# Experts, spilled blocks, last norm, embedding gate and final norm as one program

## The chip, the cores and the metric

The kernel runs on one core of a Trainium2 chip. The core has TensorE (PE) for matmuls, VectorE (DVE) and ScalarE (ACT) for elementwise work, GpSimd (POOL), and SyncE (SP), which issues DMAs. Each engine follows its own queue of instructions; they meet at semaphores. Matmul results go to PSUM, eight banks of 128 x 512 f32. All other tiles are in SBUF, 128 partitions wide. The metric is the device time of one execution in microseconds; the verdict compares medians of runs.

## What is computed

The reference is a model of two blocks over 512 tokens of 1024 features. The first is a hybrid attention mixer and a SwiGLU; the second a gated mixer, a mixture of experts and an embedding gate. Only the end of the second matters here:

```
x = x + hier_moe(rmsnorm_2(x, g_ffn), w_grp, w_exp, w1, w3, w2)
h = rmsnorm_2(x, g_ple)
x = x + sigmoid(h @ w_pg) * (p @ w_ple)
return rmsnorm_2(x, g_final)
# rmsnorm_2(x, g) = x * rsqrt(mean(x * x) + 1e-6) * g
```

`hier_moe` sends each token to 2 of 32 experts; an expert is (silu(x w1) * (x w3)) w2, with 1024 x 512, 1024 x 512 and 512 x 1024 weights.

## The kernel before, in words

The kernel is a list of stages (`build`). A stage opens a `Block`, in which each engine has its own list of instructions, and ends with a barrier of all engines. P is 128, NT 4 tiles of 128 tokens, KD 8 tiles of 128 features, CH and U 512 columns, PAIRS 16. The residual x is in `reg_b` as four tiles of 128 tokens x 1024 features.

`stage_experts` goes through 16 pairs of experts, 64 tokens each. SP loads the six weight matrices of a pair (2 MB each) into eight buffers (`b.wbuf`); a buffer is loaded again when PE is through with it. For a pair PE computes h1 and h3, DVE and ACT the gated product, PE the second product (`ex_y`), ACT (`weigh_high`, L2639) and DVE (`weigh_low`, L2647) split its weighted value in two parts, PE sends them home to their tokens with a selection matrix (`send_home`, L2656 and L2657), and DVE adds the eight results to x (`add_home`, L2663). The stages are staggered: in turn s of the loop the first products of pair s and the second of pair s - 1 are made. Behind its last weights SP loads the gate's weights `w_pg` (two halves of 2 MB), the final norm's gain row, broadcast to all partitions, and copies the products p @ w_ple (`b.pw`, 2 MB, already in SBUF) to a buffer of the ring.

`stage_spill` serves experts with more than 64 tokens. How many blocks there are is data (`b.spill`). Each engine loads the count to a register and has the code for one block in a loop inside an `If`. With these inputs the trace shows no instruction of such a block.

`stage_norm` for "n5" squares x, takes root and reciprocal, scales the rows, turns them with 32 PE transposes (L515), and ACT and DVE take the eight turned tiles out of PSUM, scaled by the gain `g_ple` per feature (L473, L507).

`stage_embedding` computes h @ w_pg in two halves of 512 output columns. A product of f32 is made of three fp32r matmuls (`product_parts`, L546 to L548): high x high, high x low, low x high. ACT makes the high part by a cast (L590 for weights, L576 for rows), DVE the low part by a subtraction (`lower`, L541). The weights come in eight units of 256 features x 512 columns, in two buffers; a unit has 24 matmuls, six for each tile of tokens, 192 in all. After the fourth and the eighth unit ACT takes the sigmoid of four banks (L2976), and DVE multiplies by `pw` (L2987) and adds to x (L2989). In its list DVE does the four gated tiles of the first half ahead of the low part of the sixth unit.

`stage_final` squares the four tiles (L3002), takes one root and one reciprocal (L3005, L3012), scales each by its factor and by the gain row on DVE (L3015), and SP stores the four tiles (L3022).

An ACT_TABLE_LOAD comes ahead of a function that is not in the loaded set; here Sqrt needs one after the others, and Sigmoid one after Sqrt.

## Time and profile before

| | us |
|---|---|
| median of 3 runs | 1934.57 |
| lowest, highest | 1934.0, 1939.59 |
| the profiled execution, its own time | 1938.65 |
| its span, first to last instruction | 1936.9 |
| PE busy in it | 1740.1 (90%) |
| DVE, ACT busy | 807.0 (42%), 516.2 (27%) |
| moved by DMA | 353.69 MB, mean 183 GB/s |

The trace names each instruction by engine, line, and the tiles it writes and reads. PE and PEld are matmuls and weight loads; a matmul's end is modelled and overlaps the next one's start, so one should count starts. A "q" behind an engine's name is its instruction queue, where barriers stand: a DRAIN is the engine's arrival at a barrier, an EVENT_SEMAPHORE the release. Times run from the span's start. The span is 1.75 us shorter than the execution's own time.

### The profile page before, as it was taken

What the parts mean: (1) busy time and instruction counts of PE and PEld (TensorE: products, weight loads), DVE (VectorE), ACT (ScalarE), POOL (GpSimd) and SP (SyncE); (2) the same over time, 40 slices, a digit from 0 to 9 for tenths busy, and PEclk for the clock granted to TensorE, in tenths of its full rate; (3) what the DMA queues carried; (4) which work ended last, traced back from release to release, by engine and by line L of the source; (5) the groups of instructions that cost most, each with busy time, mean ns of one, the idle gap of its engine ahead of it and who ended that gap; (6) DMA issues with size and microseconds to landing.
All of it is one profiled execution on the core that took longest, in us unless ns stands there. A gap on an engine that the chain in (4) does not pass through costs nothing. (4 is left out here: it accounts for less than half of the span.)

```text
span 1936.9 us, 20199 instructions
## 1 busy us (share of the span) xinstructions
PE 1740.1 (90%) x8167; PEld 1189.8 (61%) x8167; DVE 807.0 (42%) x1266; ACT 516.2 (27%) x858; POOL 46.5 (2%) x86
## 2 busy tenths in 40 slices
PE   2999989899979999999799989998998888888865
PEld 2887856546768888788688776665333434333354
DVE  4663457632652222365622553345223323232343
ACT  4212257622242222222532340423100000000032
POOL 0000000100000000000000000000200000000000
PEclk8999999989989999999899999999999999999987
DMA  9664030022512332220431111255899999999901
GB/s 356 216 264 149 1 131 1 2 96 78 174 44 91 116 98 87 98 77 32 152 110 65 37 51 44 87 236 202 359 425 426 427 428 426 426 429 427 393 1 43
DMA packets 86216, 353.69 MB, mean 183 GB/s; under 512 B 8765, under 2 KB 38121, under 8 KB 70377
## 3 DMA queue, kind: packets, MB, share of 16 engines
q1 hardware_dynamic: 83562, 343.98, 45.2%
q0 software_dynamic: 2560, 8.40, 1.1%
q8 instruction: 66, 1.08, 0.2%
q14 instruction: 28, 0.23, 0.0%
HBM read 343.93 MB, written 6.33 MB: 181 GB/s over the span
## 5 line engine op out<-in xcount | busy, mean ns | idle before, releaser
L541 DVE TENSOR_TENSOR arena<-ring,arena 128x1024 fp32r<-128x1024 f32 x120 | 146.9, 1225 | 242.3 <-ACT arena L590 223.2
L546 PE MATMUL up_ps<-h_high,arena 128*128 128x512 f32 x352 | 139.1, 395 | 6.7 <-PEq L172 6.2
L547 PE MATMUL up_ps<-arena 128*128 128x512 f32 x352 | 139.7, 397 | 0.0
L548 PE MATMUL up_ps<-h_high,arena 128*128 128x512 f32 x352 | 139.6, 397 | 0.0
L590 ACT CAST arena<-ring 128x1024 fp32r<-128x1024 f32 x82 | 85.7, 1045 | 170.2 <-PE up_ps L548 88.5
L2632 PE MATMUL ex_h<-ring,u_big_tail 128*64 128x512 f32 x512 | 116.5, 603 | 13.1 <-DMA ring<-in_w 12.8
L2632 PE MATMUL ex_h<-s_ab,u_big_tail 128*64 128x512 f32 x400 | 114.7, 596 | 11.8 <-DMA reg_a<-in_w 4.9
L2603 DVE TENSOR_TENSOR u_big_tail<-ex_x,vcol 128x512 f32<-128x512 f32 x32 | 20.6, 686 | 185.8 <-PE ex_x L2596 185.8
L2837 ACT ACTIVATE u_big_tail<-ex_h 128x512 f32<-128x512 f32 x16 | 9.6, 597 | 305.6 <-PE ex_h L2632 305.6
L2632 PEld LDWEIGHTS ex_h<-ring,u_big_tail 128*64 128x64 f32 x512 | 38.8, 138 | 76.5 <-issue 75.3
L546 PEld LDWEIGHTS up_ps<-h_high,arena 128*128 128x128 f32 x352 | 66.5, 189 | 23.4 <-issue 6.6
L2632 PEld LDWEIGHTS ex_h<-s_ab,u_big_tail 128*64 128x64 f32 x400 | 35.8, 137 | 73.3 <-issue 70.6
L547 PEld LDWEIGHTS up_ps<-arena 128*128 128x128 f32 x352 | 66.4, 189 | 16.3
L548 PEld LDWEIGHTS up_ps<-h_high,arena 128*128 128x128 f32 x352 | 66.5, 189 | 15.3
L546 PE MATMUL down_ps<-arena 128*128 128x512 f32 x176 | 68.6, 389 | 1.7 <-PEq L1767 1.7
L547 PE MATMUL down_ps<-arena 128*128 128x512 f32 x176 | 68.5, 389 | 0.0
L548 PE MATMUL down_ps<-arena 128*128 128x512 f32 x176 | 68.5, 389 | 0.0
L2632 PE MATMUL ex_y<-s_ab,u_big_tail 128*64 128x512 f32 x176 | 56.5, 594 | 13.3 <-DMA s_ab<-in_w 5.7
L2632 PE MATMUL ex_y<-ring,u_big_tail 128*64 128x512 f32 x256 | 56.6, 594 | 10.1 <-DMA ring<-in_w 10.1
L523 PE MATMUL merge_p<-s_ab,ring 128*128 128x512 f32 x128 | 59.5, 618 | 4.1 <-PEq L1162 3.1
L546 PE MATMUL p_ps<-p_h,p_w 128*128 128x512 f32 x128 | 51.8, 405 | 7.4 <-DVE p_h L541 6.8
L546 PE MATMUL p_ps<-arena,h_high 128*128 128x512 f32 x128 | 51.5, 402 | 7.6 <-PEq L172 7.6
(531 smaller groups left out, 3532.2 us busy)
## 6 DMA issues: line engine op xcount, KB each, us to landing
ring<-in_w SPq DMA_DIRECT2D x48, 2048.0 KB, 28.8
s_ab<-in_w SPq DMA_DIRECT2D x36, 2048.0 KB, 28.3
ring<-in_w_in SPq DMA_DIRECT2D x19, 2048.0 KB, 7.8
ring<-in_w_ada SPq DMA_DIRECT2D x24, 1024.0 KB, 6.7
reg_a<-in_w SPq DMA_DIRECT2D x12, 2048.0 KB, 32.1
ring<-in_w_ffn_gate SPq DMA_DIRECT2D x11, 1024.0 KB, 5.2
ring<-in_w_ffn_up SPq DMA_DIRECT2D x11, 1024.0 KB, 7.7
ring<-in_w_ffn_down SPq DMA_DIRECT2D x5, 2048.0 KB, 7.9
```

The costliest lines, as they stand in the source:

```text
L523: mm = nc.tensor.matmul(ps, w[:, k, n0:n0 + P], hT[:, k, :], start=(k == 0), stop=(k == kt - 1))
L541: return engine.tensor_tensor(lo, v, hi.bitcast(F32), ALU.subtract)
L546: nc.tensor.matmul(ps, x[0], y[0], start=start, stop=False)
L547: nc.tensor.matmul(ps, x[0], y[1], start=False, stop=False)
L548: return nc.tensor.matmul(ps, x[1], y[0], start=False, stop=stop)
L590: self.nc.scalar.copy(self.unit(u, 0), v).then_inc(self.hi, 1)
L2603: last = nc.vector.tensor_tensor(xT[:, 4 * i:4 * i + 4, :], ps[i][:].rearrange("p (k s) -> p k s", k=4), b.gcol[:, 4 * i:4 * i + 4, :], AL ...
L2632: mm = nc.tensor.matmul(ps[half, :], xT[:, k, half], ws[j][:, k, cols], start=(k == 0), stop=(k == k_end - 1))
L2837: nc.scalar.activation(b.hs, ps_h1[:], ACT.Silu).then_inc(silu, 1)
```

## The change

The stages for spilled blocks, the norm "n5", the embedding gate and the final norm become empty. Their work moves behind the pairs in the block of the experts, as the classes `Spill` and `Finish`. In short:

- Each engine loads the count of spilled blocks at the start of the loop's last turn. Behind its part of the pairs stands the same `If` over the same code as before. Where there are spilled blocks, ACT squares x again.
- SP loads the final gain row first, ahead of the experts' weights, into `scr`. The copy of `pw` goes. The two halves of `w_pg` have a semaphore each.
- The norm's gain `g_ple` goes into the weights: ACT's high part is a copy with a scale per partition, DVE's low part multiplies by it as well. The rows carry only the token's factor. ACT makes the high parts of the first two units and loads the table for Sqrt ahead of the squares.
- The squares are taken tile by tile as the experts' adds arrive. The scaled rows are turned and split tile by tile, out of PSUM: ACT the high part, DVE the low part. PE's first unit is mixed with the transposes.
- The low part of the sixth unit now stands ahead of the gated tiles of the first half. The last two units are done in the order (6,0) (6,1) (7,0) (6,2) (7,1) (6,3) (7,2) (7,3), unit and tile.
- For the final norm the squares of the first half are summed while the second half's products run, and there is a root for each tile. DVE multiplies by the gain row before the factor is known; the factor is then applied by DVE for tiles 2 and 3 and by ACT for tiles 0 and 1. They are stored in the order 2, 0, 3, 1.

```diff
 def stage_experts(b):
...
-    b.frow = b.wbuf[2][:, 0:D]
-    pw_home = b.wbuf[3].rearrange("p (t n) -> p t n", t=NT)
+    b.frow = b.scr[:, U:3 * U]
+    fin = Finish(b, pg)
...
+        spill = Spill(b, ps_x, [ps_h1, ps_h3], ps_y, [ps_t, ps_c])
+        fin.banks = [ps_h1, ps_h3, ps_t, ps_c] + ps_x + ps_y
         @block.sync
         def _(sp):
+            sp.dma_start(b.frow, a["g_final_2"].partition_broadcast(P)).then_inc(fin.row_in, 16)
             sp.wait_ge(b.ple_done, 2 * NT)
...
             sp.wait_ge(h1, PAIRS)
             for i in range(2):
-                sp.dma_start(pg[i], feature_tiles(...)[...]).then_inc(b.last_in, 16)
-            sp.wait_ge(y_done, PAIRS - 1)
-            sp.dma_start(b.frow, a["g_final_2"].partition_broadcast(P)).then_inc(b.last_in, 16)
-            sp.dma_start(pw_home, b.pw).then_inc(b.last_in, 16)
+                sp.dma_start(pg[i], feature_tiles(...)[...]).then_inc(fin.pg_in[i], 16)
+            spill.sync(sp, spill.count(sp))
+            fin.sync(sp)
         @block.gpsimd
         def _(pool):
+            nc.gpsimd.memset(fin.eps, EPS).then_inc(fin.eps_in, 1)
...
+            spill.pool(pool, spill.count(pool))
         @block.tensor
...
             for s in range(PAIRS + 1):
+                if s == PAIRS:
+                    n_spill = spill.count(pe)
...
+            spill.tensor(pe, n_spill)
+            fin.tensor(pe)
         @block.vector
...
             for s in range(PAIRS + 1):
+                if s == PAIRS:
+                    n_spill = spill.count(dve)
...
             add_all(PAIRS - 1)
+            spill.vector(dve, n_spill)
+            fin.vector(dve)
         @block.scalar
...
             for s in range(PAIRS + 1):
+                if s == PAIRS:
+                    n_spill = spill.count(act)
...
+            fin.first_weights(act)
+            for t in range(NT):
+                act.wait_ge(added, HOME * (PAIRS - 1) + 2 * t + 2)
+                last = fin.square(t)
+            last.then_inc(fin.squared, 1)
+            act.wait_ge(fin.squared, 1)
+            spill.scalar(act, n_spill, fin)
+            fin.scalar(act)
+class Spill:
...
+    def count(self, eng):
+        eng.wait_ge(self.b.spilled, 1)
+        return eng.value_load(self.b.spill[0:1, SPILL:SPILL + 1], min_val=0, max_val=SPILL)
+    def each(self, eng, n, body, after=None):
+        with eng.If(n > 0):
+            with eng.Fori(0, n) as j:
+                body(j)
+            if after is not None:
+                after()
...
+class Finish:
...
+    def act_w(self, act, u):
+        act.wait_ge(self.pg_in[u % 4 // 2], 16)
+        if u == 5:
+            act.wait_ge(self.ready, NT)
+        elif u >= 2:
+            act.wait_ge(self.used, u - 1 if u < 5 else u - 2)
+        for k in range(2):
+            v, g = self.weight(u, k)
+            last = self.nc.scalar.activation(self.w[u % 2][0][:, k, :], v, ACT.Copy, scale=g)
+        last.then_inc(self.w_hi, 1)
+    def dve_w(self, dve, u):
+        dve.wait_ge(self.w_hi, u + 1)
+        for k in range(2):
+            v, g = self.weight(u, k)
+            last = self.nc.vector.scalar_tensor_tensor(out=self.w[u % 2][1][:, k, :], in0=v, scalar=g,
+                                                       in1=self.w[u % 2][0][:, k, :].bitcast(F32), op0=ALU.mult, op1=ALU.subtract)
+        last.then_inc(self.w_lo, 1)
...
+    def first_weights(self, act):
+        self.act_w(act, 0)
+        self.act_w(act, 1)
+        act.wait_ge(self.eps_in, 1)
+        self.nc.scalar.activation(self.spare, self.eps, ACT.Sqrt)
+    def tensor(self, pe):
+        nc, b = self.nc, self.b
+        def turn(t):
+            pe.wait_ge((self.y_d, self.y_a)[t % 2], t // 2 + 1)
+            if t >= 2:
+                pe.wait_ge(self.lo, 2 * (t - 1))
+            for k in range(KD):
+                mm = nc.tensor.transpose(self.turn_bank(t, k // 4)[:, k % 4 * P:k % 4 * P + P], self.y[t][:, k * P:k * P + P], b.ident[:])
+                if k % 4 == 3:
+                    mm.then_inc(self.turned, 1)
+        def product(u, t):
+            pe.wait_ge(self.w_lo, u + 1)
+            i = u % 4
+            if u == 0:
+                pe.wait_ge(self.lo, 2 * t + 2)
+            for k in range(2):
+                mm = product_parts(nc, self.banks[u // 4 * NT + t][:], [self.h[j][:, 2 * i + k, t * P:t * P + P] for j in range(2)],
+                                   [self.w[u % 2][j][:, k, :] for j in range(2)], i == 0 and k == 0, i == 3 and k == 1)
+            if i == 3:
+                mm.then_inc(self.ready, 1)
+            return mm
+        turn(0)
+        turn(1)
+        product(0, 0)
+        turn(2)
+        product(0, 1)
+        turn(3)
+        product(0, 2)
+        product(0, 3).then_inc(self.used, 1)
+        for u in range(1, 6):
+            for t in range(NT):
+                mm = product(u, t)
+            if u != 3:
+                mm.then_inc(self.used, 1)
+        for u, t in ((6, 0), (6, 1), (7, 0), (6, 2), (7, 1), (6, 3), (7, 2), (7, 3)):
+            product(u, t)
+    def vector(self, dve):
+        nc, b = self.nc, self.b
+        def split(t):
+            for half in range(2):
+                dve.wait_ge(self.hi, 2 * t + half + 1)
+                ks = slice(4 * half, 4 * half + 4)
+                lower(nc.vector, self.h[1][:, ks, t * P:t * P + P], self.turn_bank(t, half)[:].rearrange("p (k s) -> p k s", k=4),
+                      self.h[0][:, ks, t * P:t * P + P]).then_inc(self.lo, 1)
+        def normed(t):
+            nc.vector.tensor_scalar(self.y[t], b.x[:, t, :], self.inv[:, t:t + 1], None, ALU.mult).then_inc(self.y_d, 1)
+        def gated(h, t):
+            i, cols = h * NT + t, slice(h * CH, h * CH + CH)
+            dve.wait_ge(self.gate, i + 1)
+            nc.vector.tensor_tensor(self.sg[:, i], self.sg[:, i], b.pw[:, t, cols], ALU.mult).then_inc(self.prod, 1)
+            dve.wait_ge(self.prod, i + 1)
+            nc.vector.tensor_tensor(b.x[:, t, cols], b.x[:, t, cols], self.sg[:, i], ALU.add).then_inc(self.added, 1)
+        self.dve_w(dve, 0)
+        dve.wait_ge(self.rooted, 1)
+        nc.vector.reciprocal(self.inv, self.root).then_inc(self.inverted, 1)
+        dve.wait_ge(self.inverted, 1)
+        normed(0)
+        normed(2)
+        self.dve_w(dve, 1)
+        for t in range(NT):
+            split(t)
+        for u in range(2, 6):
+            self.dve_w(dve, u)
+        for t in range(NT):
+            gated(0, t)
+        self.dve_w(dve, 6)
+        self.dve_w(dve, 7)
+        dve.wait_ge(self.sq0, NT)
+        nc.vector.tensor_scalar(self.low, self.ss0, 1.0 / D, EPS, ALU.mult, ALU.add).then_inc(self.gained, 1)
+        dve.wait_ge(self.row_in, 16)
+        for t in range(NT):
+            gated(1, t)
+            dve.wait_ge(self.added, NT + t + 1)
+            nc.vector.tensor_tensor(self.y[t], b.x[:, t, :], b.frow, ALU.mult).then_inc(self.gained, 1)
+        dve.wait_ge(self.rooted2, NT)
+        nc.vector.reciprocal(self.inv, self.root).then_inc(self.inverted2, 1)
+        dve.wait_ge(self.inverted2, 1)
+        dve.wait_ge(self.gained, NT + 1)
+        for t in (2, 3):
+            nc.vector.tensor_scalar(self.y[t], self.y[t], self.inv[:, t:t + 1], None, ALU.mult).then_inc(self.out_d, 1)
+    def scalar(self, act):
+        nc, b = self.nc, self.b
+        def normed(t):
+            nc.scalar.activation(self.y[t], b.x[:, t, :], ACT.Copy, scale=self.inv[:, t:t + 1]).then_inc(self.y_a, 1)
+        def split(t):
+            for half in range(2):
+                act.wait_ge(self.turned, 2 * t + half + 1)
+                nc.scalar.copy(self.h[0][:, 4 * half:4 * half + 4, t * P:t * P + P],
+                               self.turn_bank(t, half)[:].rearrange("p (k s) -> p k s", k=4)).then_inc(self.hi, 1)
+        def sigmoid(h, t):
+            i = h * NT + t
+            act.wait_ge(self.ready, i + 1)
+            nc.scalar.activation(self.sg[:, i], self.banks[i][:], ACT.Sigmoid).then_inc(self.gate, 1)
+        def half_square(h, t):
+            act.wait_ge(self.added, h * NT + t + 1)
+            nc.scalar.activation(self.sg[:, h * NT + t], b.x[:, t, h * CH:h * CH + CH], ACT.Square,
+                                 accum_out=(self.ss0, self.ss1)[h][:, t:t + 1]).then_inc((self.sq0, self.sq1)[h], 1)
+        nc.scalar.activation(self.root, self.ss, ACT.Sqrt, scale=1.0 / D, bias=self.eps).then_inc(self.rooted, 1)
+        act.wait_ge(self.inverted, 1)
+        normed(1)
+        split(0)
+        normed(3)
+        for t in range(1, NT):
+            split(t)
+        for u in range(2, 6):
+            self.act_w(act, u)
+        for t in range(NT):
+            sigmoid(0, t)
+        self.act_w(act, 6)
+        for t in range(NT):
+            half_square(0, t)
+        self.act_w(act, 7)
+        for t in range(NT):
+            sigmoid(1, t)
+        nc.scalar.activation(self.spare, self.eps, ACT.Sqrt)
+        act.wait_ge(self.gained, 1)
+        for t in range(NT):
+            half_square(1, t)
+            act.wait_ge(self.sq1, t + 1)
+            nc.scalar.activation(self.root[:, t:t + 1], self.ss1[:, t:t + 1], ACT.Sqrt, scale=1.0 / D,
+                                 bias=self.low[:, t:t + 1]).then_inc(self.rooted2, 1)
+        act.wait_ge(self.inverted2, 1)
+        act.wait_ge(self.gained, NT + 1)
+        for t in (0, 1):
+            nc.scalar.activation(self.y[t], self.y[t], ACT.Copy, scale=self.inv[:, t:t + 1]).then_inc(self.out_a, 1)
+    def sync(self, sp):
+        b, nc = self.b, self.nc
+        for t in (2, 0, 3, 1):
+            sp.wait_ge((self.out_a, self.out_d)[t // 2], t % 2 + 1)
+            sp.dma_start(b.out[0, t * P:(t + 1) * P, :], self.y[t]).then_inc(self.stored, 16)
+        sp.wait_ge(self.stored, 16 * NT)
 def stage_spill(b):
-    ...
+    return
 def stage_combine(b):
-    ...
+    return
 def stage_embedding(b):
-    ...
+    return
 def stage_final(b):
-    ...
+    return
```

## Rows read from the trace of the kernel before

**Rows 1.** The page's 40 slices of the span: DMA busy tenths, and GB/s:

```profile
DMA  9664030022512332220431111255899999999901
GB/s 356 216 264 149 1 131 1 2 96 78 174 44 91 116 98 87 98 77 32 152 110 65 37 51 44 87 236 202 359 425 426 427 428 426 426 429 427 393 1 43
```

**Rows 2.** Chain of waits: shares by line, then start us, us:

```profile
by line: ACT u_big L3002 0.2%; DVE u_big L3015 0.2%; ACT L3005 0.1%; DVEq L2998 0.1%; ACTq L2998 0.0%; DVE small L3012 0.0%; issue 0.0%
...
1921.69 4.27 ACT u_big L3002 x8
```

**Rows 3.** Instructions of L2684, the experts' barrier: duration ns, first and last start us:

```profile
L2684 ACTq EVENT_SEMAPHORE  x1: 17/17/17, 1844.0 to 1844.0; - x1
```

**Rows 4.** Instructions of L2855, the spilled blocks' barrier:

```profile
L2855 ACTq DRAIN  x1: 14/14/14, 1844.9 to 1844.9; - x1
...
L2855 DVEq DRAIN  x1: 19/19/19, 1845.3 to 1845.3; - x1
L2855 PEldq DRAIN  x1: 13/13/13, 1848.8 to 1848.8; - x1
```

**Rows 5.** Timeline of ACT from 1800: start us, us, instruction [idle before]:

```profile
1835.33 1.27 ACT L2639 ACTIVATE y_hi_tail<-ex_y,share 128x512 fp32r<-128x512 f32 x2 [23.42 <-PE ex_y L2632]
...
1851.30 1.28 ACT L467 ACT_TABLE_LOAD   x1
1852.59 0.21 ACT L467 ACTIVATE small<-small 128x4 f32<-128x4 f32 x1
...
1915.36 2.06 ACT L2976 ACTIVATE s_ab<-em_g 128x512 f32<-128x512 f32 x4 [9.78 <-PE em_g L548]
```

**Rows 6.** Timeline of DVE from 1800:

```profile
1827.42 0.68 DVE L2818 COPY u_big_tail<-ex_t 128x512 f32<-128x512 f32 x1
...
1843.06 0.68 DVE L2663 TENSOR_TENSOR reg_b<-reg_b,ex_x 128x512 f32<-128x512 f32 x1
```

**Rows 7.** Timeline of PE from 1818:

```profile
1825.63 0.63 PE L2760 MATMUL ex_t<-ident,u_big_tail 128*128 128x128 f32 x4
...
1841.66 0.39 PE L2657 MATMUL ex_x<-y_lo_tail,pick_tail 128*128 128x512 f32 x1
...
1864.90 0.77 PE L546 MATMUL em_g<-em_w,em_h 128*128 128x512 f32 x1 [5.42 <-DVE em_h L541]
...
1894.85 0.39 PE L548 MATMUL em_g<-em_w,em_h 128*128 128x512 f32 x1
1897.07 0.50 PE L546 MATMUL em_g<-em_w,em_h 128*128 128x512 f32 x1 [1.83 <-DVE em_w L541]
...
1914.93 0.39 PE L548 MATMUL em_g<-em_w,em_h 128*128 128x512 f32 x1
```

**Rows 8.** Windows: busy us of each engine, PEclk the granted clock:

```profile
1847.00:1848.00 1.00, 0.00 (x0) 0.00 (x0) 0.00 (x0) 0.00 (x0) 0.00 (x0) 0.58 0.00 0
1858.00:1859.00 1.00, 1.00 (x12) 1.00 (x11) 0.25 (x1) 0.14 (x1) 0.00 (x0) 1.00 0.00 0
1865.00:1871.00 6.00, 6.00 (x14) 4.66 (x15) 5.10 (x8) 2.92 (x5) 0.00 (x0) 0.50 0.00 0
1872.00:1894.00 22.00, 22.00 (x99) 18.22 (x98) 7.11 (x9) 7.43 (x9) 0.00 (x0) 1.00 0.00 1
1898.00:1902.00 4.00, 4.00 (x13) 3.10 (x12) 0.15 (x1) 0.00 (x0) 0.00 (x0) 0.57 0.00 0
```

**Rows 9.** Groups by line and form, 1835 to 1937: busy us, mean ns:

```profile
L497 DVE TENSOR_SCALAR u_big_tail<-reg_b,small 128x1024 f32<-128x1024 f32 x2 | 1.4, 751 | 0.0
L2647 DVE SCALAR_TENSOR_TENSOR y_lo_tail<-ex_y,share,y_hi_tail 128x512 fp32r<-128x512 f32 x2 | 1.4, 746 | 8.1 <-ACT y_hi_tail L2639 8.1
```

**Rows 10.** Timeline of SP from 1150:

```profile
1333.51 0.35 SPq L2573 DMA_DIRECT2D reg_a<-in_w  x1
1357.79 10.24 SPq L2573 DMA_DIRECT2D s_ab<-in_w  x3
...
1929.03 3.92 SPq L3022 DMA_DIRECT2D out<-u_big  x4
```

More of the change, by code:

```diff
@@ L415, in stage_norm @@
                residual_row=None, save=None):
-    if made is not None or name in ("n2", "n3", "n4"):
+    if made is not None or name in ("n2", "n3", "n4", "n5"):
         return
@@ L2992, in stage_final @@
-def stage_final(b):
-    nc = b.nc
-    y = b.u_big[:, 0:NT * D].rearrange("p (t d) -> p t d", t=NT)
-    ss = b.small[:, 0:4]
-    sq, var, root, inv, done, stored = (b.sem(f"fi_{n}") for n in ("sq", "var", "root", "inv", "done", "stored"))
-    with nc.Block() as block:
-        @block.scalar
-        def _(act):
-            for t in range(NT):
-                last = nc.scalar.activation(y[:, t, :], b.x[:, t, :], ACT.Square, accum_out=ss[:, t:t + 1])
-            last.then_inc(sq, 1)
-            act.wait_ge(var, 1)
-            nc.scalar.activation(ss, ss, ACT.Sqrt).then_inc(root, 1)
-        @block.vector
-        def _(dve):
-            dve.wait_ge(sq, 1)
-            nc.vector.tensor_scalar(ss, ss, 1.0 / D, EPS, ALU.mult, ALU.add).then_inc(var, 1)
-            dve.wait_ge(root, 1)
-            nc.vector.reciprocal(ss, ss).then_inc(inv, 1)
-            dve.wait_ge(inv, 1)
-            for t in range(NT):
-                nc.vector.scalar_tensor_tensor(out=y[:, t, :], in0=b.x[:, t, :], scalar=ss[:, t:t + 1], in1=b.frow,
-                                               op0=ALU.mult, op1=ALU.mult).then_inc(done, 1)
-        @block.sync
-        def _(sp):
-            for t in range(NT):
-                sp.wait_ge(done, t + 1)
-                sp.dma_start(b.out[0, t * P:(t + 1) * P, :], y[:, t, :]).then_inc(stored, 16)
-            sp.wait_ge(stored, 16 * NT)
```

247 lines of the change are left out of this document (120 added, 127 removed).

## The prediction

> **What bounds the kernel now.** I read the page's slices first: from slice 29 to 37 the DMA engines are busy 9 tenths and more [rows 1]. That is the experts' weights coming in. There the kernel is bound by DMA, at some 426 GB/s in the second row; but in slice 38 the transfers have stopped, and what the change rewrites lies there and behind. So I read the chain of waits backwards: it holds only the final norm, behind a barrier [rows 2]. The stretch that the change rewrites must be followed by the timelines of the engines, from ACT's high part of the last pair's output (weigh_high) at 1835.33 [rows 5] and the last add of the experts on DVE, 1843.06 + 0.68 = 1843.74 [rows 6], to the span's end at 1936.9. These 93.2 us are five blocks in a row, each closed by a barrier:
> - 1843.74 to 1849.1: the spilled blocks, of which there are none. The barrier that closes the experts lets ACT go at 1844.0 [rows 3]; ACT reaches the next one at 1844.9, DVE at 1845.3, PE at 1848.8 [rows 4]. All wait for PE.
> - to 1861.8: the norm: squares, a table load (1851.30), the root, four scalings, 32 transposes, scaled copies [rows 5].
> - 1861.8 to 1864.90: the embedding gate splits weights and rows in two; PE starts at 1864.90 [rows 7].
> - 1864.90 to 1915.3: 192 matmuls. A stretch of full clock holds 22.00 us for 97 of them (the 99 of the row count two that cross its edges), 0.227 each; one at the lower clock has 14 in 6.00 us, 0.427 each [rows 8]. 192 x 0.227 = 43.5. The rest is 6.1 us of low clock at the start (up to 1871.0: 6.1 x 0.47 = 2.9; 0.47 is 0.20/0.427), a wait of 2.0 for DVE at 1895.1 [rows 7], and a second fall of the clock behind that wait, at 1898.3, 3.4 us long (a mean of 0.57 over the 4 us [rows 8]; 1.6). Sum 50.0; the rows have 1864.90 to 1915.16.
> - 1915.3 to 1936.9: sigmoids 1915.36 [rows 5], gating, final norm, outputs from 1929.03 [rows 10]. 21.6 us.
>
> **The front of the new tail, part by part.** Everything up to 1835.33 stays. The profile then gives each engine's order.
> ACT: weigh_high ends 1836.6. The first two weight units are four scaled copies 128x512, of the kind of which two took 1.27 [rows 5], until 1839.1; the gate's weights are queued right behind the last experts' and DMA has nothing left in slice 38 [rows 1]. Table load 1.28 [rows 5] and a root, 1840.6. These hide under the experts' last adds. Then four squares with sums (four took 4.27 [rows 2]); the fourth can start when its adds are in, 1843.74, and ends at 1845.0 with its accumulator read. So squares and table load cost 1.3 behind the adds, not 3.6 behind a barrier.
> The branch over the spilled blocks is still taken. Load and branch together took ACT 0.9 and DVE 1.3 [rows 3, 4]; the load is now made earlier, at idle time. I take 0.5 for ACT (bounds 0 and 0.9). DVE has it beside ACT's last square, then the low halves of the first unit (two of 0.746 [rows 9]), until 1845.9.
> Root 0.2, reciprocal 0.2: 1846.1. Rows of tile 0 scaled on DVE, 0.75 [rows 9], 1846.9; tile 2, 1847.6; second weights, 1849.1. ACT scales tile 1 beside that. PE turns tile 0 from 1847.0 and tile 1: 16 transposes, 12 of which fit in 1.00 us at full clock [rows 8], so at half of it until about 1849.8. DVE is the last here: it can split tile 0 only after the second weights: two subtractions of 0.68, as the DVE rows of [rows 6], 1850.5. **First product at 1850.5 against 1864.90: 14.4 us.** Bounds for what I cannot see, DVE's waits between engines: 1.0 either way.
> PE pays for the branch too: it took 4.8 us for load and branch [rows 3, 4]. Its sends are dispatched by 1841.7 [rows 7], so even 4.8 puts it at 1846.5, before tile 0 is there at 1846.9: nothing, as long as the rest of the chain isn't shorter.
> The Trainium skill ("Runtime: NRT & Kernel Launch", Instruction fetch mechanics) says that a taken branch to a target outside the window of two fetched pages stalls for a fetch. The gap between PE's 4.8 us and ACT's 0.9 agrees, since PE's skipped body is by far the longest. The bodies of ACT and DVE are short, and by that rule they would go free; a body that crosses the edge of a page would not, which is rival A.
>
> **Inside the experts.** The early load of the count stands in PE's queue ahead of the last pair. PE's four transposes begin at 1825.63 and take 0.63, DVE copies their result only at 1827.42, behind its adds [rows 6, 7]: a slack of 1.2 us. ACT's 0.9 fits in it: cost 0. If all of PE's 4.8 is the load, it costs 3.6; I keep this end for the range. On ACT, DVE and SP the load falls into waits. The final gain row moves from behind the experts to SP's queue ahead of the first weights. SP issues nothing between 1333.51 and 1357.79 [rows 10] and can issue it when the router's barrier opens at about 1350: no cost; if it does push the saturated stretch, half a megabyte at 426 GB/s [rows 1] is 1.2 us. The copy of the products (2 MB) goes: it ran behind the last needed weights, gain 0.
>
> **The products.** 192 x 0.227 = 43.5 again. Transposes of tiles 2 and 3 now stand between them: 16 x 0.09 [rows 8] = 1.4. Low clock: PE has stopped from 1842.05 to 1847.0; before, the clock fell in the microsecond from 1847 [rows 8] with the same beginning, so I let it be low, and rise 6.1 us after the first product as it did before: 2.9. Bounds: none of it (-2.9), or one more fall as at 1898.3 (+1.6). **The wait of 2.0 and its low clock of 1.6 go:** the weights of the second half's start (unit 4 and 5) are now split ahead of the gating. What is late next? Count from the end of unit 3, with 5.44 us a unit. ACT: weights 1.1, table load 1.28, four sigmoids of 0.6, +4.8; next weights when unit 4 is done, +6.6. DVE gates 8 x 0.68 from +3.1 to +8.5, unit 6's low halves +9.9, needed at +10.9. ACT's half squares end at +9.4; unit 7's weights wait for unit 5, +12.0, low halves +13.5; PE, which does (6,0) and (6,1) first, asks at +13.6. It fits by 0.1, so I count no wait, and up to 0.5 for the range. PE ends 1850.5 + 43.5 + 1.4 + 2.9 = 1898.3; the last sigmoid starts at 1898.5 (before: 1915.36).
>
> **The tail.** Sigmoid 0.6, 1899.1; table load 1.28, 1900.4; then for each tile a half square, its sum and a root: 0.6 + 0.15 + 0.2 = 0.95, four times, 1904.2. DVE's own work (for the last tile two of 0.68, and the product with the gain row of about 1.3) ends at 1902.9, beside it. Reciprocal, first tile scaled in 0.75: first output issued at 1905.2, 6.7 after the sigmoid's start; before it was 13.7 (1915.36 to 1929.03 [rows 5, 10]). **Gain 7.0.** The outputs themselves do not get faster: before, the tiles came every 1.2 us, and the span ended 7.9 after the first issue; 2 MB at 426 GB/s [rows 1] are 4.9 of it. Now they come within 1.5 us and queue: 1905.2 + 7.9 = 1913.1.
> The Trainium skill ("ScalarE: Activation LUTs", What ACT_TABLE_LOAD costs) puts about 1.38 us of drain beside each load. Here the load at 1851.30 is followed by its root at 1852.59, so no drain shows. With it the tail would be 1.4 longer, 1914.5 in place of 1913.1.
>
> **Sum.** 1936.9 - 1913.1 = 23.8: 14.4 (front) + 3.6 (wait and second fall) - 1.4 (transposes among the products) + 7.0 (tail) + 0.2 (rounding). The profiled execution took 1938.65, so 1914.9 by its own scale. That execution is 4.1 above the median of the runs shown, 1934.57; the difference taken from the median gives 1910.8, and I say **1911**.
>
> **Rivals.**
> A. The branch costs ACT or DVE what it cost PE. Each is on the path to the first product: 4.8 - 0.5 = 4.3 more, 1915. For it: PE's row. Against: ACT's and DVE's rows, with nearly the same bodies. 0.15.
> B. New waits of PE between units, as the 0.1 us of margin at unit 7, or tile by tile in unit 0, where each tile now passes ACT, DVE and PE in turn. One such wait of 2.0 cost 3.6 with the clock behind it; two cost 7.2: 1915 to 1918. For it: every handover is tighter. Against: PE's 5.44 a unit stand against 2.6 of ACT and DVE. 0.15.
> C. The tail is as long as before, because the roots by tile sit behind table load and gating, or the load of the count holds up PE for its 3.6: 1915 to 1918. 0.08.
> D. Slower than before: PE stays at the lower clock through the products. 192 x 0.427 = 82.0, 35.6 more than my 46.4: 1947. It decides from 51 us of extra low clock (51 x 0.47 = 24). For it: after each of the last three pauses the clock fell. Against: it came back within 7 us each time in which PE then worked on. 0.04.
> E. The change does not take effect: a wait not seen (the weights of the gate, the gain row) holds the merged block so that most of the gain goes: 1925 to 1936. 0.05, a third of it within 0.3% of before.
> My own forecast, 1907 to 1915, has 0.53.
>
> **Range.** Low end: no low clock (-2.9) and 1 us from the front, 1907, less 1 for the spread of runs (1934.0 to 1939.59 before): 1906. High end: A or B with a little more, 1918. It leaves out D, E and parts of B and C. What tells a change from none is 0.3%, 5.8 us. Faster: 0.93, same: 0.02, slower: 0.05.
>
> **What would show it.** The first product of the gate about 6.8 us after the experts' last add (before: 21.2). PE unbroken until the last product, 48 us. No fall of the clock after the first. Table load directly behind the last sigmoid, four half squares and roots in about 3.8 us, first output 6.7 us behind the last sigmoid's start. Wrong, if ACT's root starts later than 1.5 us behind its last square, if PE's transposes at the last pair slip past DVE's copy, or if a unit's first matmul waits for DVE.

## The result, and the profile after

The changed kernel took 1919.06 us (median of 5 runs, 1913.68 to 1923.1), the kernel before 1939.59 in the 5 runs beside it: ratio 0.9894 [0.9869, 0.9919], 20.5 us less. I had said 1911, from 1906 to 1918, so the time lies above the range. The profiled execution took 1913.68; its page begins

```profile
span 1911.8 us, 20177 instructions
...
DMA  9664030022512223221422020237699999999931
GB/s 355 220 256 157 10 132 1 2 88 88 176 44 88 88 88 103 87 108 45 152 91 88 1 88 29 79 123 317 241 426 424 428 427 427 426 427 426 428 124 44
```

The saturated stretch is as it was ([rows 1]: nine slices of 9 tenths at some 426 GB/s). The chain of waits, which held the final norm alone before [rows 2], now leads back through the gate's products and the experts' to the transfer of their weights (shares of the span by engine):

```profile
DMA 15%; PE 12%; ACT 1%; DVE 1%; issue 0%; SPq 0%; ACTq 0%; DVEq 0%
```

ACT's timeline (start us, us, instruction, idle before and what ended it) holds most of the answer to [rows 5]:

```profile
1835.37 1.26 ACT L2641 ACTIVATE y_hi_tail<-ex_y,share 128x512 fp32r<-128x512 f32 x2 [23.48 <-PE ex_y L2634]
1836.53 2.55 ACT L3021 ACTIVATE em_w<-s_ab,vcol 128x512 fp32r<-128x512 f32 x4
1839.09 1.28 ACT L3042 ACT_TABLE_LOAD   x1
...
1844.77 0.19 ACT L3036 ACTIVATION_READ_ACCUMULATOR ring<-reg_b 128x1 f32 x1
1845.15 1.28 ACT L3155 ACT_TABLE_LOAD   x1 [0.19 <-ACT ring L3036]
1846.44 0.30 ACT L3155 ACTIVATE small<-small 128x4 f32<-128x4 f32 x1
...
1897.92 0.60 ACT L3148 ACTIVATE s_ab<-ex_y 128x512 f32<-128x512 f32 x1 [0.76 <-PE ex_y L549]
1898.54 1.28 ACT L3172 ACT_TABLE_LOAD   x1
1899.83 0.20 ACT L3172 ACTIVATE small<-small 128x1 f32<-128x1 f32 x1
...
1903.50 0.30 ACT L3177 ACTIVATE small<-small 128x1 f32<-128x1 f32 x1
1904.04 2.19 ACT L3182 ACTIVATE u_big_tail<-u_big_tail,small 128x1024 f32<-128x1024 f32 x2 [0.24 <-DVE small L3127]
```

The first two weight units, the first table load and three of the four squares lie under the experts' adds; the last square ends 1.2 behind them. But a second load of the same table (1845.15) stands behind the branch. The last adds on DVE, the PE rows that answer to [rows 7], and SP's outputs:

```profile
1827.46 0.68 DVE L2830 COPY u_big_tail<-ex_t 128x512 f32<-128x512 f32 x1
...
1843.09 0.68 DVE L2665 TENSOR_TENSOR reg_b<-reg_b,ex_x 128x512 f32<-128x512 f32 x1
...
1849.64 1.47 DVE L542 TENSOR_TENSOR em_h<-ex_x,em_h 128x512 fp32r<-128x512 f32 x2
```

```profile
1825.69 0.71 PE L2768 MATMUL ex_t<-ident,u_big_tail 128*128 128x128 f32 x4
...
1847.80 1.97 PE L3052 MATMUL ex_x<-ident,u_big_tail 128*128 128x128 f32 x8 [5.74 <-DVE u_big_tail L3095]
1849.56 1.57 PE L3052 MATMUL ex_y<-ident,u_big_tail 128*128 128x128 f32 x8
1851.26 0.47 PE L547 MATMUL ex_h<-em_w,em_h 128*128 128x512 f32 x1
...
1857.66 0.47 PE L547 MATMUL ex_c<-em_w,em_h 128*128 128x512 f32 x1 [0.26 <-DVE em_h L542]
...
1889.43 0.50 PE L547 MATMUL ex_x<-em_w,em_h 128*128 128x512 f32 x1 [0.22 <-DVE em_w L3028]
```

```profile
1904.82 2.90 SPq L3188 DMA_DIRECT2D out<-u_big_tail  x4
```

The windows that answer to [rows 8] (busy us of PE, PEld, DVE, ACT, POOL, then granted clock) show a lower clock under the first transposes, and the full clock from there to the last product, also over 1865 to 1871, where before had 0.50:

```profile
1848.00:1851.00 3.00, 3.00 (x16) 2.89 (x15) 2.91 (x5) 1.92 (x4) 0.00 (x0) 0.56 0.00 0
1851.00:1854.00 3.00, 2.87 (x18) 2.42 (x17) 1.42 (x4) 2.04 (x5) 0.00 (x0) 1.00 0.00 0
...
1865.00:1871.00 6.00, 6.00 (x28) 4.96 (x27) 1.42 (x2) 1.90 (x4) 0.00 (x0) 1.00 0.01 3
```

To compare kernels whose experts end at different times, I count from the end of the experts' last add (1843.09 + 0.68 = 1843.77 here, [rows 6] before) and call what follows, up to the span's end, the tail. The closing sigmoid is the first that starts behind the last product. In the kernels before it is the first of four in a row (the fourth starts 1.45 later), in the changed ones the last of all. The first two columns are times of the execution, the others count from the end of the last add; all in us:

| kernel, profiled execution | its time | last add | first transpose | first product | closing sigmoid | first output | tail |
|---|---|---|---|---|---|---|---|
| before | 1938.65 | 1843.74 | 10.50 | 21.16 | 71.62 | 85.29 | 93.2 |
| before again (e8) | 1937.16 | 1845.47 | 10.11 | 21.04 | 68.42 | 82.09 | 89.9 |
| before, third (e9) | 1933.88 | 1842.17 | 10.10 | 21.05 | 68.43 | 82.11 | 89.9 |
| changed | 1913.68 | 1843.77 | 4.03 | 7.49 | 54.15 | 61.05 | 68.0 |
| changed again (e1) | 1912.57 | 1842.63 | 4.02 | 7.48 | 54.17 | 61.07 | 68.0 |
| changed, third (e10) | 1917.79 | 1847.88 | 4.02 | 7.48 | 54.15 | 61.05 | 68.0 |
| changed, row late (e11) | 1924.09 | 1854.16 | 4.02 | 7.48 | 54.16 | 61.05 | 68.0 |
| changed, no spill code (e2) | 1915.61 | 1846.99 | 2.57 | 5.84 | 53.03 | 59.92 | 66.9 |
| before, no spill code (e3) | 1932.42 | 1845.36 | 5.45 | 17.03 | 64.72 | 78.38 | 85.3 |
| before, unit 5 early (e4) | 1932.13 | 1842.72 | 10.12 | 20.93 | 66.13 | 79.81 | 87.7 |
| changed, unit 5 late (e6) | 1918.44 | 1840.73 | 4.02 | 7.48 | 61.94 | 68.84 | 75.8 |
| changed, norm in one (e7) | 1915.12 | 1841.40 | 4.02 | 7.48 | 55.36 | 64.88 | 71.8 |
| early branch, short tail (e5) | 1909.16 | 1842.27 | 2.57 | 5.84 | 52.92 | 58.03 | 64.9 |
| the same again (e12) | 1912.67 | 1845.77 | 2.56 | 5.84 | 52.92 | 58.03 | 65.0 |

The tail is the same within 0.1 us in four profiles of the changed kernel (the late row's among them); the last add is not, by 1842.6 to 1854.2. So the last column can judge an edit to a few tenths, where run times need dozens of runs. It has a limit: where the clock falls otherwise, the tail moves too, as in the first profile of before (93.2 for 89.9) and in e7, whose code up to the closing sigmoid is that of the changed kernel and which comes there 1.2 later.

### The profile page after: what moved, and what is told of

Same layout as the page of the kernel before. It is cut to its first block and busy times, and to the rows that moved or that the text cites. A ratio compares the mean times of both kernels' runs of the same rounds, so it can differ in the third digit from the quotient of the medians.

```text
span 1911.8 us, 20177 instructions
## 1 busy us (share of the span) xinstructions
PE 1736.2 (91%) x8167; PEld 1186.8 (62%) x8167; DVE 805.1 (42%) x1267; ACT 524.2 (27%) x882; POOL 46.6 (2%) x87
## 5 line engine op out<-in xcount | busy, mean ns | idle before, releaser
L548 PEld LDWEIGHTS up_ps<-arena 128*128 128x128 f32 x352 | 66.4, 189 | 16.3
L2641 ACT ACTIVATE y_hi_tail<-ex_y,share 128x512 fp32r<-128x512 f32 x32 | 20.2, 683 | 141.6 <-PE ex_y L2634 141.6
```

Source lines behind the costliest of these rows:

```text
L548: nc.tensor.matmul(ps, x[0], y[1], start=False, stop=False)
L2641: last = nc.scalar.activation(b.y_hi[:, h * CH:(h + 1) * CH], ps[h][:], ACT.Copy, scale=share)
```

## The experiments

**Both kernels again (e8, e9 before; e1, e10 changed).** No edit. They ask how much of the difference belongs to the kernels and how much to one draw.

> The changed kernel once more, unaltered, against the kernel before. The two profiled executions differ by 25.0 us (1938.65 and 1913.68), all of it behind the experts' last add (1843.74 and 1843.77), but the medians by 20.5 only. Theory T1 (base): the change saves about 25 us in every run; both kernels scatter by 9 us through time at the lower clock ahead of the tail, and the first median of before, 1934.57, was a low draw. Then the new runs' means differ by 24 to 26, and times of one kernel follow the mean granted clock of the run (0.001 less of it is 2 x 0.001 x 1930 x 0.47 = 1.8 us). Rival T2: the tail itself gives back some 5 us in most runs, by a clock that falls in the products; then the means differ by 19 to 21, and a profile of a run of 1919 shows the experts' last add at 1843.8 and a longer tail.

> The kernel before, unaltered, for a second profile. So far the saving is 25.1 us between two profiles, but 20.4 between the means (28 runs of before, 10 of the changed kernel). Theory: the first profile of before had the longest tail, 93.2 from the experts' last add, with low clock of 6.1 us at the first product and 3.4 behind the wait; the same tail is shorter by 1.6 to 4 us in other runs, as it was in the variant without spill code (85.3 + 5.0 = 90.3, no second fall), so this one has 89 to 92. Rival: the tail is 93.2 again, and the means differ from it by chance in the stretch ahead.

> The kernel before for a third profile. From the experts' last add to the end it took 93.2 and 89.9 us, with 19 and 14 us at the lower clock from 1840 on; the changed kernel 68.0 twice, with 4 and 7. Theory: before's tail lies between 87 and 94, by how the clock's falls meet the norm and the products; the tail's saving is thus 19 to 26 and not the fixed 25.1 of the first pair. Rival: 93.2 again.

> The changed kernel for a third profile, with five more runs. Theory: tail 68.0 again within 0.5, because its pause of PE is short and always the same; the mean over now 15 runs is 20 to 23 us below that of before. Rival: the tail grows by 3 or more in the runs above 1918.

The changed kernel's tail comes again, in a run of 1917.79 too; the first profile of before does not. Its tail is 3.2 longer than in both others. So neither theory of e1 holds: the saving is not 25 in every run, and the changed kernel's tail doesn't grow in the longer runs. PE's rows of the second profile show the same wait as [rows 7], and its window the full clock where [rows 8] has 0.57:

```profile
1866.51 0.76 PE L546 MATMUL em_g<-em_w,em_h 128*128 128x512 f32 x1 [5.42 <-DVE em_h L541]
...
1869.61 0.40 PE L547 MATMUL em_g<-em_w,em_h 128*128 128x512 f32 x1
...
1897.23 0.50 PE L546 MATMUL em_g<-em_w,em_h 128*128 128x512 f32 x1 [1.82 <-DVE em_w L541]
```

```profile
1898.00:1902.00 4.00, 4.00 (x19) 3.29 (x18) 0.32 (x1) 0.00 (x0) 0.00 (x0) 1.00 0.00 0
```

The wait belongs to the kernel, the fall behind it does not (1.6 of the 3.2); e3 below has the wait and no fall behind it as well. The rest is the start: the low clock ends 3.1 us behind the first product here (rows of 0.63 give way to 0.40 at 1869.6), 6.1 in the first profile [rows 8], 3.0 x 0.47 = 1.4. The times: changed 1916.1 (5 runs, 1910.23 to 1919.91) against 1937.33 (23 runs), ratio 0.9891 [0.9867, 0.9915]; changed 1914.28 (5 runs) against 1938.18 (11 runs), 0.9873 [0.9852, 0.9895]. Over all runs, on several chips, before has 46 with median 1938.5 and mean 1938.4 (standard deviation 3.3), changed 15 with median 1916.1 and mean 1916.3 (3.4): 22.1 less, with a standard error of 1.0.

**Without the code for spilled blocks (e2, e3).** With these inputs there are no spilled blocks; the kernels leave out the load of their count, the branch and the skipped body, nothing that is computed here. In the changed kernel, and the whole stage in the one before:

```
-                if s == PAIRS:
-                    n_spill = spill.count(act)      (and so for each engine)
...
-            spill.scalar(act, n_spill, fin)
...
 def stage_spill(b):
+    return
```

> The changed kernel without the code for spilled blocks: no count, no branch (there are none to be done with these inputs). It tells what the branch costs where it stands. Profile after: ACT's second table load at 1845.15 (1.28) stands behind the branch although the first, at 1839.09, loaded the same table. Theory: the branch makes the table's state unknown and costs the second load; without it the first product starts 1.4 to 1.6 us earlier (1.28 + 0.19), and the span is shorter by that. Rival: the load comes with the first use of Sqrt with four columns whatever stands ahead; then only 0.2 goes. PE's own 4.8 us is hidden in both.

> The kernel before without the stage for spilled blocks. Theory: it stood on the path in one piece, with its barrier, for PE's load and branch: 1844.0 to 1849.0, so 5.0 us less. Rival: part of it comes back, because the clock's level in the norm and the products depends on when PE starts: 2 to 5 us less.

ACT's timeline of the changed kernel without it: the root stands right behind the last sum, with the same early table load and no second one.

```profile
1847.98 0.19 ACT L3025 ACTIVATION_READ_ACCUMULATOR ring<-reg_b 128x1 f32 x1
1848.20 0.30 ACT L3144 ACTIVATE small<-small 128x4 f32<-128x4 f32 x1
```

So the branch costs the first product 1.64 us (7.48 to 5.84), nearly all of it ACT's: 1.28 for the reload, 0.19 idle. Of this only 1.1 reaches the end (68.0 to 66.9). The rest goes to the clock, as the rows under e5 show: the earlier first product meets the lower clock. In before, the first transposes come 4.65 earlier (10.10 to 5.45), which is PE's way to the barrier of [rows 4], and the tail is 4.6 shorter than in e8 and e9. Only 3.7 of that stands at the first output (82.1 to 78.4). The other 0.9 comes behind it, where the last output lands sooner (3.0 us from its issue for 3.9), though the four are issued at the same distances.

The branch itself stands in the traces. The first three rows are the kernel before (the load of the count, and the branch); the next is the changed kernel, and the last the one of e5, which keeps PE's branch:

```profile
L2862 PEldq TENSOR_LOAD <-spill x1: 489/489/489, 1844.1 to 1844.1; - x1
L2863 ACTq COMPARE_BRANCH  x1: 45/45/45, 1844.8 to 1844.8; - x1
L2863 PEldq COMPARE_BRANCH  x1: 3727/3727/3727, 1845.0 to 1845.0; - x1
...
L2889 PEldq COMPARE_BRANCH  x1: 3388/3388/3388, 1840.8 to 1840.8; - x1
...
L2889 PEldq COMPARE_BRANCH  x1: 3705/3705/3705, 1839.3 to 1839.3; - x1
```

So 3.7 of PE's 4.8 us are the branch instruction (0.07 on DVE), and the load of the count is 0.5 of it. In the changed kernel PE's branch ends at 1844.2, 3.6 ahead of the first transpose. In e5 the transposes start at 2.57 with PE's branch in the program, and in e2 at 2.57 without it: PE's part is hidden in both places.

The run times say less: 1915.69 and 0.9892 [0.9868, 0.9915] for the first (the changed kernel beside it: 0.9891), 0.9988 [0.9972, 1.0004] for the second (12 runs, mean 1934.7 against 1937.3).

**Unit 5's weights early, in the kernel before (e4).** Both parts of unit 5 are split ahead of the first sigmoids and the gating:

```
-                parts.act_w(act, u + 1)
+                if u != 4:
+                    parts.act_w(act, u + 1)
+                if u == 3:
+                    parts.act_w(act, 5)       (the same for dve_w)
```

> The kernel before with one part of the change: both parts of the sixth unit's weights are made ahead of the sigmoids and the gated tiles of the first half. Theory: PE's wait of 2.0 us at 1895 goes, and with it the fall of the clock at 1898.3 (1.6 us): 3.6 us less. Rival: the clock falls there without the wait too; then 2.0 less. DVE's gating comes 1.2 us later and still ends ahead of the seventh unit.

PE no longer waits there, and the tail is 2.25 shorter than in e8 and e9 (5.5 than in the first profile). The wait was worth 2.0 to 2.3, without a second fall behind it; my 3.6 had added one. Run times: 0.9992 [0.9976, 1.0008], not to be told from nothing at this size.

**The low part of unit 5 late, in the changed kernel (e6).** The converse:

```
-        for u in range(2, 6):
+        for u in range(2, 5):
             self.dve_w(dve, u)
         for t in range(NT):
             gated(0, t)
+        self.dve_w(dve, 5)
```

> The changed kernel with one part undone: the low part of the sixth unit stands behind the gated tiles of the first half again. Measured from the experts' last add to the end (68.0 in the changed kernel, whatever the run's total). Theory: PE waits about 2 us ahead of that unit, 70.0; with a fall of the clock behind the wait as in the first profile of before, 71.6. Rival: none of it, since the gating starts earlier against PE than before: 68.0.

The tail grew by 7.75, more than expected. PE's rows and a window behind the wait:

```profile
1877.62 0.39 PE L549 MATMUL ex_y<-em_w,em_h 128*128 128x512 f32 x1
1882.73 0.80 PE L547 MATMUL ex_x<-em_w,em_h 128*128 128x512 f32 x1 [4.72 <-DVE em_w L3028]
```

```profile
1884.00:1890.00 6.00, 6.00 (x18) 4.72 (x18) 0.01 (x1) 0.00 (x0) 0.00 (x0) 0.61 0.00 0
```

ACT starts the sigmoids only behind unit 5's high part and the table load, DVE starts gating at 1875.95 and comes to unit 5's low halves at 1881.27; so the wait is 4.9 (1877.85 to 1882.73) and not 2.0. Behind it PE is at the lower clock for some 5.8 us, 5.8 x 0.47 = 2.7; the two make 7.6 of the 7.75. This is one profile. In it one line's place in DVE's order costs a third of what the whole change saves.

**The final norm in one piece, in the changed kernel (e7).** Squares of all four tiles, one table load and root, four fused scalings, as before:

```
         for t in range(NT):
             gated(1, t)
-            dve.wait_ge(self.added, NT + t + 1)
-            nc.vector.tensor_tensor(self.y[t], b.x[:, t, :], b.frow, ALU.mult).then_inc(self.gained, 1)
...
-        for t in (2, 3):
-            nc.vector.tensor_scalar(self.y[t], self.y[t], self.inv[:, t:t + 1], None, ALU.mult).then_inc(self.out_d, 1)
+        for t in range(NT):
+            nc.vector.scalar_tensor_tensor(out=self.y[t], in0=b.x[:, t, :], scalar=self.inv[:, t:t + 1], in1=b.frow,
+                                           op0=ALU.mult, op1=ALU.mult).then_inc(self.out_d, 1)
...
-        nc.scalar.activation(self.spare, self.eps, ACT.Sqrt)
...
+        act.wait_ge(self.added, 2 * NT)
         for t in range(NT):
-            half_square(1, t)
...
+            last = nc.scalar.activation(self.y[t], b.x[:, t, :], ACT.Square, accum_out=self.ss1[:, t:t + 1])
...
+        nc.scalar.activation(self.root, self.ss1, ACT.Sqrt, scale=1.0 / D, bias=self.eps).then_inc(self.rooted2, 1)
...
-        for t in (2, 0, 3, 1):
+        for t in range(NT):
```

> The changed kernel with the final norm in one piece as before: four squares of whole tiles behind the last add, one root, four tiles scaled with gain on DVE, stored in order. Theory: first output 13.7 us behind the last sigmoid's start in place of 6.9, 6.8 us more: from the experts' last add to the end 74.8. Rival: half of it, because the outputs now come one by one and no longer queue: the last 7.0 after the first issue stay 7.9, so 75.7; or the barrier that is gone makes it 74.4.

```profile
1906.28 3.92 SPq L3181 DMA_DIRECT2D out<-u_big_tail  x4
```

From the closing sigmoid's start to the first output 9.52 us, against 6.90 changed and 13.67 before. So 2.6 of the gain come from the norm by tiles. The other 4.2 are there with the old norm too: since the last two units now end their banks tile by tile, three tiles are gated under PE, and only the last is left behind the last product, where before four sigmoids stood in a row [rows 5]. DVE's last add of the gating ends 2.05 behind the closing sigmoid's start, for 6.03 before; the barrier that is gone makes 0.3 more. The tail as a whole is 3.8 longer: 2.6, and 1.2 ahead of the closing sigmoid, where the low clock lasted longer than in the changed kernel, to about 2.7 us behind the first product (0.54 over 1846 to 1852). The edit doesn't touch that part; whether a draw or the shorter program shifted the fall, one profile can't tell.

```profile
1846.00:1852.00 6.00, 6.00 (x26) 5.17 (x25) 3.93 (x7) 3.18 (x5) 0.00 (x0) 0.54 0.00 0
```

**The final gain row late (e11).** The move of the row back behind the gate's weights, in the changed kernel:

```
-            sp.dma_start(b.frow, a["g_final_2"].partition_broadcast(P))
             sp.wait_ge(b.ple_done, 2 * NT)
...
+            sp.dma_start(b.frow, a["g_final_2"].partition_broadcast(P))
             spill.sync(sp, spill.count(sp))
```

> The changed kernel with the load of the final gain row back behind the gate's weights. Forecast: nothing (0.0 in the tail; the row is there some 50 us ahead of its use in both places), and ahead of the tail nothing that stands out of its scatter. Rival: half a megabyte less in front of the experts' weights lets the first ones land 1.2 us sooner.

The tail is 68.0, as ever: the row's place costs it nothing. The run itself was long (1924.09), all of it ahead of the tail. Of its 10.4 us more, 6.5 were there at the first product of the FFN's up matrix (573.2 against 566.7), some 780 us before the row is issued in the changed kernel (1350.59). One draw, whose cause I don't know.

**A version that beats both (e5, e12).** The rows pointed to two things: ACT's branch can be taken ahead of the first weights, where ACT has time, so that the table loaded behind it stays; and in the end the last tile is all that has to wait.

```
+            spill.scalar(act, n_spill, fin)
             fin.first_weights(act)
             for t in range(NT):
...
-            spill.scalar(act, n_spill, fin)
             fin.scalar(act)
...
-        self.each(act, n, body, again)
+        self.each(act, n, body)
...
-        for t in range(NT):
+        for t in range(2):
             gated(1, t)
...
+        gated(1, 2)
+        gated(1, 3)
+        nc.vector.tensor_tensor(self.y[2], b.x[:, 2, :], b.frow, ALU.mult).then_inc(self.gained, 1)
...
+        nc.vector.tensor_scalar(self.y[2], self.y[2], self.inv[:, 2:3], None, ALU.mult).then_inc(self.out_d, 1)
+        dve.wait_ge(self.added, 2 * NT)
+        nc.vector.scalar_tensor_tensor(out=self.y[3], in0=b.x[:, 3, :], scalar=self.inv[:, 3:4], in1=b.frow,
+                                       op0=ALU.mult, op1=ALU.mult).then_inc(self.out_d, 1)
...
-        for t in range(NT):
-            sigmoid(1, t)
+        sigmoid(1, 0)
+        sigmoid(1, 1)
+        half_square(1, 0)
+        sigmoid(1, 2)
+        half_square(1, 1)
+        sigmoid(1, 3)
         nc.scalar.activation(self.spare, self.eps, ACT.Sqrt)
+        half_square(1, 2)
+        half_square(1, 3)
```

The four roots now stand in a row behind the last half square. Since ACT's branch comes ahead of the squares, they needn't be taken again behind spilled blocks.

> A version meant to beat both: ACT takes its branch over the spilled blocks ahead of the first weights (the squares are then made once, behind it), so the table is loaded once; and in the last step ACT takes the half squares of tiles 0 and 1 between the sigmoids, DVE gates tile 3 ahead of tile 2's gain row, and scales tile 3 with its gain row in one instruction. Theory: from the changed kernel's profile, root 1.5 us earlier (no second load, 0.2 of branch), and first output at 2.1 us earlier within the tail (1904.8 to 1902.7), outputs still limited by their transfer; from the experts' last add to the end 68.0 - 1.5 - 2.1 = 64.4. Rival: the front's gain is lost because PE's transposes and DVE's second weights do not move with the root (the clock is then lower for longer): 66.0. In medians 3 us less is within the scatter.

> The version with ACT's early branch and the shorter last step once more, with five runs. From the experts' last add to the end it took 64.9, against 68.0 of the changed kernel. Theory: 64.9 again within 0.5, and a mean 3 us (2 to 5) below the changed kernel's in the same call. Rival: no difference of the means, since the scatter ahead of the tail hides it: within 1.5.

```profile
1843.26 0.19 ACT L3031 ACTIVATION_READ_ACCUMULATOR ring<-reg_b 128x1 f32 x1
1843.48 0.30 ACT L3155 ACTIVATE small<-small 128x4 f32<-128x4 f32 x1
...
1895.81 1.28 ACT L3176 ACT_TABLE_LOAD   x1
...
1898.43 0.84 ACT L3182 ACTIVATE small<-small 128x1 f32<-128x1 f32 x4
```

The second load is gone, as in e2, but here with the branch still in the program. So its cause is the branch's place between the first load and the root; what put the load there (the program as built, or the engine) the traces don't show. Behind the closing sigmoid the first output comes after 5.11 instead of 6.90. The front's 1.64 leaves 1.23 at the closing sigmoid, because the first product now starts inside the low clock (PE's rows: 0.77 and 0.55 where the changed kernel has 0.47 and 0.40):

```profile
1848.11 0.77 PE L547 MATMUL ex_h<-em_w,em_h 128*128 128x512 f32 x1 [0.27 <-DVE em_h L542]
1848.67 0.55 PE L548 MATMUL ex_h<-em_w,em_h 128*128 128x512 f32 x1
```

Tails 64.9 and 65.0. Times: 1909.55 (4 runs) against 1939.72, ratio 0.9852 [0.9832, 0.9872]; 1912.22 (6 runs) against 1938.18, 0.9865 [0.9842, 0.9888]. All ten have the mean 1912.0, 4.3 below the changed kernel's 15 (standard error 1.3) and 26.4 below before's 46; the tails put it 3.0 below the changed kernel.

## Why the prediction was right and wrong

**The base.** "The difference taken from the median gives 1910.8": this is the step that failed. The three runs shown had the median 1934.57, and I took the profiled execution for 4.1 too long. It was not: 46 runs have the median 1938.5, and 1938.65 lay on it. The same 23.8 taken from 1938.5 gives 1914.7, beside a median of 1916.1 over all 15 runs. The five runs of the result drew 1919.06, 3.0 above that. So the 8.3 between 1910.8 and 1919.06 are 3.9 of base, 1.4 of size and 3.0 of the result's own draw. Without either of the larger two the time would have lain in the range. A base 3.9 too low was bad luck in part: of medians of three drawn from the 46 runs, one in eleven is as low. But with single runs that spread by 3.3 it had to be allowed for, and my range held nothing for the spread at its high end, only "less 1" at the low one.

**The size.** Between the two first profiles the spans differ by 25.1, so 23.8 seemed short; against the tails of e8 and e9 it is 21.9, and the means of all runs differ by 22.1. The prediction's "last sigmoid" of before, 1915.36, is the first of the closing four; the four parts below count from it as well:

| | predicted | first profiles | against e8, e9 | 
|---|---|---|---|
| last add to first product | 14.4 | 13.7 | 13.6 |
| first product to closing sigmoid | 2.4 | 3.8 | 0.7 |
| closing sigmoid to first output | 7.0 | 6.8 | 6.8 |
| first output to end | 0 | 0.9 | 0.9 |
| sum | 23.8 | 25.1 | 21.9 |

The second row holds the error of size. "The wait of 2.0 and its low clock of 1.6 go" took the fall at 1898.3 for a consequence of the wait. Three more profiles (e8, e9, e3) have the wait without the fall, and e4 takes the wait away for 2.25. A price of the clock read once, in one execution, isn't the kernel's. In e6 a longer wait (4.7) in the same place did come with a fall. The same holds for the low clock at the first product, 6.1 us in the first profile and 3.1 in e8. In the other direction I charged the products 2.9 of low clock; they paid none: the clock was low under the 16 transposes from 1847.8, and full by 1851, when the first product began. This, and the 0.9 of the last row, which I had at 0, kept the sum near the truth: two errors that happened to offset the others.

**The front.** First product 7.49 behind the last add; I had 6.8. Weights, the first three squares and the first table load hid as said. PE's load of the count, ahead of four transposes, cost 0, as said: DVE's copy at 1827.46 starts 16.3 ahead of the end of the last add, as in before and in e2, which has no load. The four transposes take 0.71 in this profile and 0.63 in e1 and e10, so even that much isn't the load's. The end that I kept for the range, "all of PE's 4.8 is the load", is ruled out by the rows under e3, and PE's branch was over before tile 0 came. ACT's branch was costed at 0.5 and bounded by 0.9. It cost 1.6, for a reason outside these bounds: behind the join of the branch the table is loaded again, though the program had loaded it at 1839.09. That is rival A's place at a third of its 4.8, and by another mechanism. The trace has 1.29 from the load's start to the root behind it, at 1845.15 and again at 1898.54; the Trainium skill ("ScalarE: Activation LUTs", What ACT_TABLE_LOAD costs) puts a drain of about 1.38 beside each load, and no such drain shows in either place.

**The products.** From the first product to the closing sigmoid 46.7 us; I had 48.0. "It fits by 0.1, so I count no wait": PE waited in unit 0 and ahead of unit 7 (rows at 1857.66 and 1889.43, idle 0.26 and 0.22). Counted by starts, as the 2.0 was, that is 0.4 each. It is rival B at a fifth of its 3.6, and the clock stayed full behind both. Rival D did not happen: PE's clock came back 3.2 us after the first transpose.

**The tail.** 6.9 from the closing sigmoid to the first output, against 6.7 said. The size was right and the credit was not: the sum was worked out from the roots by tile, and e7 gives them 2.6 of the gain; the other 4.2 are the banks that close tile by tile, which the sum used (one sigmoid of 0.6, one tile's gating) and didn't name. The outputs end 7.0 behind the first issue, where I said 7.9. They are issued closer together now (2.90 us for four, 3.92 before [rows 10]), but that isn't the reason: e3 and e7 issue theirs over 3.92 as well and end 7.0 and 6.9 behind the first, where before, e8, e9 and e4 have 7.9. The last landing makes it, 3.9 us there and 3.0 in e3 and e7. Why, stays open.

**Rivals C and E** did not happen: the span ended at 1911.8, for 1913.1 said.

**Where a run's own spread comes from.** The time of one kernel goes with the time that PE spends at the lower clock (span times the clock's distance from 1, doubled): over 41 runs of before the correlation is 0.86, with 0.28 us of run time for each us at the lower clock. That is less than the 0.47 that a product loses for each us at the lower clock; the rest isn't accounted for. In the six profiles of the two kernels 52 to 66 us at the lower clock lie ahead of 560 us, 34 to 40 between 560 and 1340, and 3 to 20 between 1840 and the last product. The start of the FFN's up matrix alone moves from 563.3 to 573.2 over the fourteen profiles. So most of the spread arises ahead of the part that was changed. That the clock causes it is the likeliest reading, not shown.

**Open.** Why the first profile of before drew a second fall; why the last output lands later in four profiles; what PE does in the 3.7 us of its branch; what made e11's run late; whether the low clock at the first transposes could be kept away by giving PE something to do between 1842.1 and 1847.8. No such version was tried.

## What to carry to other kernels

Take the difference from the time with the most runs behind it, not from the smallest sample, and give the base an error of its own, at both ends of the range: here it was larger than that of the sum. When a wait is followed by a fall of the clock, price the wait from the row and the fall as a chance, unless a second profile shows it too. Here an activation table loaded ahead of a branch was loaded again behind it; take the branch first. And when an edit is worth a few us in a kernel whose runs spread over ten, compare the stretch from a fixed event to the end, in two profiles each at least: it repeated to 0.1 us in four profiles of the changed kernel, but one of three of before was 3.2 off.

## What the runs showed of the hardware that I had not expected

- A second ACT_TABLE_LOAD of the same table behind the join of a branch: 1.28 us and 0.19 idle, gone when the branch stands ahead of the first load (e5) or is absent (e2).
- The skipped branch is one instruction of 3.4 to 3.7 us on PE, 0.07 on DVE and 0.045 on ACT. It is worth 4.65 us at before's first transposes, with the load, and nothing in e5, whose transposes start 2.57 behind the last add as in e2, which has no branch.
- Four outputs of 0.5 MB, issued over 3.92 us, end 7.9 behind the first issue in four profiles and 6.9 to 7.0 in two (e3, e7), by the landing of the last alone.
- A wait of 1.8 left the clock full in three executions (1.00 behind it in e8, e9 and e3) and was followed by a mean of 0.57 over 4 us in one; a wait of 4.7 was followed by 0.61 over 6 us, at the first product behind it already low.
- A start 1.64 earlier gave only 1.1 to 1.2 at the closing sigmoid: the first products then ran at the lower clock (0.77 for one of 0.47).
